# Which pairs of a feed-forward run as Strassen products, and in what order: one pair more, and a new order for the first

## The chip, the cores and the metric

The kernel runs on one core of a Trainium2 chip. The metric is the device time of one execution in microseconds, the median of several runs; smaller is better.

## The reference, cut to what matters

One layer over 640 tokens (512 of a prompt, 128 of eight running streams) of width 1024: a feed-forward, a mixer, a second feed-forward, each behind a modulated RMS norm, and a final norm. The change touches the two feed-forwards alone.

```python
D_MODEL, D_FF = 1024, 2816
def swiglu(h, w1, w2):
    g, u = jnp.split(h @ w1, 2, axis=-1)
    return (jax.nn.silu(g) * u) @ w2
...
        hn = modulate(rmsnorm(x, norm_g[l, 0]), sh1, sc1)
        x = x + 0.5 * g1[:, None, :] * swiglu(hn, ffn_w1[l, 0], ffn_w2[l, 0])
...
        hn = modulate(rmsnorm(x, norm_g[l, 2]), sh3, sc3)
        x = x + 0.5 * g3[:, None, :] * swiglu(hn, ffn_w1[l, 1], ffn_w2[l, 1])
```

## The kernel before, in words

Everything is held transposed: a tile is 128 features by 640 tokens, two halves of 320 columns. Every product of float32 numbers is made of three fast ones: a number is split into a high part (a rounded copy, made by ScalarE) and a low part (the rest, a subtraction on VectorE), and TensorE adds high times high, high times low and low times high.

**A feed-forward** is `ffn(fi)` for fi 0 and 1. Its 2816 hidden features are 22 **pairs** (`p`, 0 to 21): one 128-wide column block of g and the same of u. The pairs stand in six parts (`PARTS` 4, 4, 4, 4, 3, 3); after the pairs of a part come eight "down" products (`first_downs`, `down`) which multiply the part's hidden tiles by w2 and are added to x. A pair's weights come as one job of 1 MB into one of two buffers `raw0`, `raw1`; SyncE loads the next job when the low parts of the last block of the job before the previous one have been made (`load_job`, a wait on `blk_lo`). The weights are cut into **blocks** of 128x512. Block b has its high and low part in one of seven slots; ScalarE makes the high part (`blk`, L1569) when TensorE has done with block b - 7 and counts `blk_hi`; VectorE makes the low part (`blk`, L2142) and counts `blk_lo`; TensorE counts `blk_done`.

**Two kinds of pair.** The first `PLAIN` = 3 pairs are plain: four blocks, 8 k-tiles x 3 terms x 2 halves x 2 outputs = 96 matmuls of 320 columns (L1056, L1075). From pair 3 on a pair is in Strassen's form (Winograd's variant, `wino_pair`): the pair is a 2x2 product (g and u by first and second half of the tokens; the inner dimension split in two), and seven products of 12 matmuls each (`product`, L1087) take the place of eight. For this VectorE makes four sums of weight blocks per pair (`s_add`, L2105: s1w, a difference in the raw buffer, s2w, and another in the raw buffer, counted by `s_sum`), and, once per feed-forward, sums of activations: `t_sums(fi, kk)` for kk 0 to 3 (four operations of 128x320 each, L2278 to L2283) with their splits `t_high`, `t_low`, `t1_high`, `t1_low`, counted by `t_ready`. The products are added up in three PSUM banks: x (a half of pC, in turn for even and odd pairs), z (a half of acc0) and w (the other half of acc0). ScalarE copies partial states of the banks out (the **snapshots** s0, p7, s1, s2, L1750, counted by `snap`), and VectorE adds these to banks: c21, c22, c11 (L2350, L2353, L2357, counted by `c_sum`). Then come silu on ScalarE (L1762, L1764), the product with u on VectorE (L2362, `hidp_done`), and its split, `hid_high` (L1719) and `hid_low` (L2306).

**What sets the order.** Each engine works strictly through its own list, and these lists are written out by hand in the `plain_pair`, `wino_pair` and `ffn` of the four engines; semaphores join them. In `wino_pair` ScalarE and VectorE make the blocks of the next pair (b + 7 to b + 13) in between the snapshots and sums of this one. Two waits of TensorE matter here: the second product of a pair writes acc0 and waits until c11 of the pair before has been made (`c_sum` 3n; the z bank and w bank are read by c21 and c11), and the third product, on the x bank, waits for the snapshot s0 of the same pair (`snap` 4n + 1).

**Duos.** In some pairs (`DUO_ROWS`; in the first feed-forward after pairs 1, 2, 5, ...; in the second after 3 and 7) TensorE also computes two chunks of the conditioning vectors: `duo_rows` (L986) after the pair, `duo_row` on ScalarE (L1702, last in its list for the pair, counted by `d_row`), then two transposes `duo_cols` (L997) within the next pair, which wait for `d_row`, and `duo_sum` on VectorE.

Of the kernel before, what the change touches and what calls it, by code (L numbers as in the profile page):

```python
# [8 lines left out]
ALU = mybir.AluOpType  # L9
# [19 lines left out]
PLAIN = 3  # L29
KQ = KD // 2  # L30
# [54 lines left out]
def trunk_program(nc, x_prompt, x_sample, state_ssm, state_conv, c_prompt, c_sample, w_ada, b_ada, norm_g,  # L85
# [347 lines left out]
    SLOT0, RAW0 = (2, 4), (0, 1)  # L433
    BLOCK = {}
    for p, b in enumerate(BLK_PAIR):
        for j in range(4 if p < PLAIN else SLOTS):
            BLOCK[b + j] = ("plain" if p < PLAIN else "wino", p, j)
# [20 lines left out]
    def slot_of(fi, b, lo, cols):  # L458
        return slots[(b + SLOT0[fi]) % SLOTS][:, lo * WB:lo * WB + cols]
# [20 lines left out]
    S_AT = {1: 2, 2: 3, 4: 1, 6: 4}  # L480
# [367 lines left out]
    def _(pe):  # L848
# [231 lines left out]
        def product(fi, b, out, block, first):  # L1080
# [3 lines left out]
            for kk in range(KQ):  # L1084
                a_hi, a_lo = block(kk)
# [5 lines left out]
        def wino_pair(fi, p, cols):  # L1091
# [14 lines left out]
            if cols is not None and p == PLAIN:  # L1106
                duo_cols(cols)
# [5 lines left out]
            if p == PLAIN:  # L1113
                pe.wait_ge(t_ready, 6 * fi + KQ + 2)
# [420 lines left out]
    def _(act):  # L1535
# [18 lines left out]
        def blk(fi, b):  # L1554
# [4 lines left out]
            if kind == "wino" and j in S_AT:  # L1559
                act.wait_ge(s_sum, 4 * wino_before(fi, p) + S_AT[j])  # L1560
# [160 lines left out]
        def plain_pair(fi, p):  # L1721

            b = BLK_PAIR[p]
            if p == 1:
                t_high(fi, 1)
# [4 lines left out]
            if p == 1:  # L1730
                t_high(fi, 2)
            if p == 2:
                t_high(fi, 3)
            blk(fi, b + 7)
            blk(fi, b + 8)
            act.wait_ge(blk_done, fi * NB + b + 4)
            if p == PLAIN - 1:
                t1_high(fi)
            hid_high(fi, p)
            blk(fi, b + 9)  # L1740
            blk(fi, b + 10)

        def wino_pair(fi, p):
# [8 lines left out]
            blk(fi, b + 7)  # L1752
            snapshot("p7", z_bank, 2)
            blk(fi, b + 8)
            snapshot("s1", x, 3)
            blk(fi, b + 9)
            blk(fi, b + 10)
            snapshot("s2", x, 5)
# [287 lines left out]
    def _(dve):  # L2046
# [779 lines left out]
```

## Time and profile before

| | us |
|---|---|
| median of 3 runs (lowest to highest) | 1442.93 (1442.92 to 1444.68) |
| the profiled execution | 1445.51 |
| its span in the trace | 1443.9 |
| TensorE busy in matmuls | 1422.3 (99%) |
| VectorE busy | 1014.5 (70%) |
| ScalarE busy | 663.6 (46%) |
| GpSimd busy | 71.5 (5%) |

The span is from the first to the last instruction in the trace; the device time holds some 1.6 us more around it. The shares are means over the whole span. A timeline row gives start, length, engine, line, operation, tiles, count, and in brackets how long the engine was idle before it and what ended that. Operations on one engine overlap a little, so that what a step costs in a dense stretch is the distance from its start to the next start, not its own length. The first feed-forward's part 0 lies at 22 to 124 us, the second's at 986 to 1076 us.

### The profile page before, as it was taken

The page shows a single profiled execution, that of the slowest core. Times are in us where ns is not written, and L with a number is a line of the kernel's source. Part 1 is how long each engine was busy: PE and PEld are TensorE (multiplying, and loading weights), DVE is VectorE, ACT ScalarE, POOL GpSimd, SP SyncE. Part 2 cuts the span into 40 slices and gives each one's busy share as a digit, 9 for nine tenths or more (in the row PEclk, how much of TensorE's full clock was granted, in tenths as well). Part 3 has the DMA queues.
Part 4 walks back from the last instruction along what each step waited for, and adds up shares of the span by engine and source line. Part 5 has one row for each costly group of instructions (what it writes and reads, how often), then busy time and mean ns, then how long its engine had stood idle before and what let it go on. Part 6 is the DMA issues. An engine that isn't in the chain of part 4 may idle for free.

```text
span 1443.9 us, 25671 instructions
## 1 busy us (share of the span) xinstructions
PE 1422.3 (99%) x10202; PEld 1372.2 (95%) x10202; DVE 1014.5 (70%) x1742; ACT 663.6 (46%) x1186; POOL 71.5 (5%) x121
## 2 busy tenths in 40 slices
PE   7999999999999999999999999999999999999998
PEld 6899999999999999999789999998999999999997
DVE  5767677676776776667886567557767676767776
ACT  5543525253435444666825453226425253444354
POOL 3100000000000130000100000004000000000001
PEclk9999999999999999999999999999999999999999
DMA  9752434444344612231362222444324233231222
GB/s 319 213 187 61 159 105 146 117 147 147 110 139 132 184 30 74 74 93 54 98 187 77 67 73 63 133 143 122 110 56 143 67 88 88 71 105 52 81 74 74
DMA packets 219564, 161.02 MB, mean 112 GB/s; under 512 B 6858, under 2 KB 204678, under 8 KB 219458
## 3 DMA queue, kind: packets, MB, share of 16 engines
q1 hardware_dynamic: 217490, 153.89, 35.7%
q0 software_dynamic: 1696, 5.56, 1.3%
q8 instruction: 74, 1.21, 0.4%
q14 instruction: 32, 0.26, 0.1%
q10 hardware_dynamic: 272, 0.10, 0.0%
HBM read 151.50 MB, written 8.03 MB: 110 GB/s over the span
## 4 chain that ended last, share of the span: by engine, by line
PE 92%; DVE 3%; DMA 2%; ACT 1%; POOL 1%; issue 1%; SPq 0%; DVEq 0%; ACTq 0%; POOLq 0%
PE acc L864 25%; PE acc L1196 19%; PE pC L1087 18%; PE acc L1087 14%; PE acc L1075 4%; PE pB L986 2%; PE acc L1145 2%; PE pC L1336 1%; DMA ada_raw<-in_w_ada 1%; DMA raw<-in_ffn_w 1%; PE pB L945 1%; PE pB L1321 1%; PE pC L1471 1%; PE pC L1355 1%; PE acc L881 0%
## 5 line engine op out<-in xcount | busy, mean ns | idle before, releaser
L1569 ACT ACTIVATE slot<-raw 128x512 fp32r<-128x512 f32 (+1 forms) x310 | 189.7, 616 | 239.4 <-PE acc L1196 137.8
L2142 DVE TENSOR_TENSOR slot<-raw,slot 128x512 fp32r<-128x512 f32 (+1 forms) x310 | 208.6, 677 | 53.8 <-ACT slot L1569 51.3
L1196 PE MATMUL acc<-hid_hi,slot 128*128 128x320 f32 x1240 | 238.5, 310 | 0.0
L1087 PE MATMUL pC<-hn_hi,slot 128*128 128x320 f32 x912 | 216.3, 309 | 0.0
L1196 PEld LDWEIGHTS acc<-hid_hi,slot 128*128 128x128 f32 x1240 | 195.1, 188 | 2.9 <-issue 2.1
L864 PE MATMUL acc<-hn_hi,whi 128*128 128x320 f32 x672 | 161.5, 322 | 0.0
L1087 PEld LDWEIGHTS pC<-hn_hi,slot 128*128 128x128 f32 x912 | 156.2, 188 | 2.5 <-issue 2.5
L864 PE MATMUL acc<-hn_hi,wlo 128*128 128x320 f32 x672 | 153.5, 310 | 0.0
L864 PE MATMUL acc<-hn_lo,whi 128*128 128x320 f32 x672 | 153.5, 310 | 0.0
L1087 PE MATMUL acc<-tT,slot 128*128 128x320 f32 x912 | 146.3, 309 | 0.0
L1196 PE MATMUL acc<-hid_lo,slot 128*128 128x320 f32 x620 | 142.0, 308 | 0.0
L1087 PE MATMUL pC<-hn_lo,slot 128*128 128x320 f32 x456 | 140.8, 309 | 0.0
L1087 PEld LDWEIGHTS acc<-tT,slot 128*128 128x128 f32 x912 | 136.5, 188 | 0.0
L864 PEld LDWEIGHTS acc<-hn_hi,whi 128*128 128x128 f32 x672 | 112.4, 189 | 6.4 <-issue 5.9
L864 PEld LDWEIGHTS acc<-hn_lo,whi 128*128 128x128 f32 x672 | 112.9, 189 | 0.0
L864 PEld LDWEIGHTS acc<-hn_hi,wlo 128*128 128x128 f32 x672 | 112.8, 189 | 0.0
L1196 PEld LDWEIGHTS acc<-hid_lo,slot 128*128 128x128 f32 x620 | 103.8, 188 | 0.0
L2086 DVE TENSOR_TENSOR xadd<-acc,gate 128x128 f32<-128x128 f32 x95 | 27.6, 290 | 90.4 <-PE acc L1196 77.4
L2056 DVE TENSOR_TENSOR wlo<-wraw,whi 128x1024 fp32r<-128x1024 f32 x50 | 61.0, 1222 | 38.5 <-ACT whi L1549 37.9
L1087 PEld LDWEIGHTS pC<-hn_lo,slot 128*128 128x128 f32 x456 | 85.5, 188 | 0.0
L2080 DVE SCALAR_TENSOR_TENSOR xT<-acc,gate,xT 128x320 f32<-128x320 f32 (+1 forms) x190 | 82.6, 475 | 0.2 <-PE acc L881 0.2
L1087 PE MATMUL pC<-tT,slot 128*128 128x320 f32 x456 | 73.2, 309 | 0.0
(389 smaller groups left out, 2404.3 us busy)
## 6 DMA issues: line engine op xcount, KB each, us to landing
raw<-in_ffn_w SPq DMA_DIRECT2D x86, 512.0 KB, 5.1
sraw<-in_w_ada SPq DMA_DIRECT2D x26, 1024.0 KB, 7.2
wraw<-in_w_in SPq DMA_DIRECT2D x36, 512.0 KB, 3.6
raw<-in_ffn_w SPq DMA_DIRECT2D x16, 1024.0 KB, 5.0
ada_raw<-in_w_ada SPq DMA_DIRECT2D x8, 1024.0 KB, 11.0
wraw<-in_w_out SPq DMA_DIRECT2D x16, 512.0 KB, 4.2
raw<-in_ffn_w SPq DMA_DIRECT2D x8, 768.0 KB, 4.4
sraw<-in_w_ada_final SPq DMA_DIRECT2D x6, 1024.0 KB, 7.5
```

The source lines that it names most:

```text
L864: last = mm(acc[p][:, h * BANK:h * BANK + HALF], w[:, k, :], a[:, k * TOK + h * HALF:k * TOK + (h + 1) * HALF], start=(k == 0 and t == 0), ...
L945: last = nc.tensor.transpose(out[:, c * P:(c + 1) * P], src[:, c * P:(c + 1) * P], ident[:, :])
L986: last = mm(q_rows[lane_of(duo)][q * QUAD:(q + 1) * QUAD, :], c_f32[:, k, :], kxn(duo_raw(duo, j), KD, ADA_COLS)[:, k, :], start=(kk == 0) ...
L1075: last = mm(half(acc[d], h), w[:, kk * P:(kk + 1) * P], a[:, k * TOK + h * HALF:k * TOK + (h + 1) * HALF], start=(k == 0 and t == 0), stop ...
L1087: last = mm(out, w[:, kk * P:(kk + 1) * P], a, start=(first and kk == 0 and t == 0), stop=(kk == KQ - 1 and t == 2), skip_group_check=not ...
L1145: last = mm(a[h], w[t // 2][:, k, :], (hid_hi, hid_lo)[t % 2][:, k * TOK + h * HALF:k * TOK + (h + 1) * HALF], start=(k == 0 and t == 0), ...
L1196: last = mm(a[h], w[t // 2][:, k, :], (hid_hi, hid_lo)[t % 2][:, k * TOK + h * HALF:k * TOK + (h + 1) * HALF], start=(k == 0 and t == 0), ...
L1569: A(slot_as(fi, b, 0), source_of(fi, b), ACT.Copy).then_inc(blk_hi, 1)
L2056: V.tensor_tensor(out=weights(n, i, 1, w), in0=wraw[p][:, 0:w], in1=weights(n, i, 0, w).bitcast(F32), op=ALU.subtract).then_inc(wlo_done, 1)
L2080: return V.scalar_tensor_tensor(out=x[:, s:e], in0=a[s // HALF][:, p:p + e - s], scalar=gate[:, q, f * GRP:f * GRP + 1], in1=x[:, s:e], op ...
L2086: V.tensor_tensor(out=by_stream(xadd[:, SEQ:TOK]), in0=by_stream(a[1][:, SEQ - HALF:HALF]), in1=g, op=ALU.mult)
L2142: V.tensor_tensor(out=slot_as(fi, b, 1), in0=source_of(fi, b), in1=slot_as(fi, b, 0).bitcast(F32), op=ALU.subtract).then_inc(blk_lo, 1)
```

## The change

`PLAIN` goes from 3 to 2: pair 2 is a Strassen pair as well, in both feed-forwards. As the sums of activations must now be there one pair earlier, they are made during pairs 0 and 1, and pair 2, the first Strassen pair, has an order of its own: first the two products that need no activation sum (b11 and b21), then t2 (waiting tile by tile), t3, t1, t4 and b22; its blocks are numbered in that order (`FIRST_ROLES`), and its snapshots follow in the order in which the banks must be free (s0, s1, p7, s2). `hid_high` and `hid_low` of pair 1 and its product with u move behind the start of pair 2. The slots are numbered anew so that the last blocks fall where they fell.

```diff
-PLAIN = 3
+PLAIN = 2
...
-    SLOT0, RAW0 = (2, 4), (0, 1)
+    SLOT_OF, RAW0 = ((0, 1, 2, 3, 6, 4, 5), (4, 5, 6, 0, 1, 2, 3)), (0, 1)
+    FIRST_ROLES = (0, 5, 2, 1, 4, 3, 6)
...
@@ TensorE, wino_pair
             if p == PLAIN:
                 pe.wait_ge(silu_done, fi * N_PAIR + p)
-                pe.wait_ge(t_ready, 6 * fi + KQ)
-            elif PART_OF[p] != PART_OF[p - 1]:
+                product(fi, b + 1, w_bank, b21, True)
+                if cols is not None:
+                    duo_cols(cols)
+                pe.wait_ge(snap, 4 * n + 1)
+                product(fi, b + 2, x, t2, False, 6 * fi)
+                product(fi, b + 3, z_bank, t3, True)
+                pe.wait_ge(snap, 4 * n + 2)
+                pe.wait_ge(t_ready, 6 * fi + KQ + 2)
+                product(fi, b + 4, x, t1, False)
+                pe.wait_ge(snap, 4 * n + 3)
+                product(fi, b + 5, z_bank, t4, False)
+                pe.wait_ge(snap, 4 * n + 4)
+                product(fi, b + 6, x, b22, False)
+                return
+            if PART_OF[p] != PART_OF[p - 1]:
...
@@ ScalarE, wino_pair
             snapshot("s0", x, 1)
+            if p == PLAIN:
+                blk(fi, b + 3)
+                blk(fi, b + 4)
+                snapshot("s1", x, 3)
+                blk(fi, b + 5)
+                blk(fi, b + 6)
+                snapshot("p7", z_bank, 4)
+                hid_high(fi, p - 1)
+                blk(fi, b + 7)
+                snapshot("s2", x, 5)
+                blk(fi, b + 8)
+                blk(fi, b + 9)
+                blk(fi, b + 10)
...
@@ VectorE, wino_pair
+            if p == PLAIN:
+                blk(fi, b + 4)
+                gated_pair(fi, p - 1)
+                blk(fi, b + 5)
+                hid_low(fi, p - 1)
+                blk(fi, b + 6)
+                if cols is not None:
+                    duo_sum(cols)
+                blk(fi, b + 7)
+                dve.wait_ge(blk_done, fi * NB + b + 6)
...
             V.tensor_tensor(out=c21, in0=snaps["s1"], in1=z_bank, op=ALU.add).then_inc(c_sum, 1)
+            if p == PLAIN:
+                blk(fi, b + 8)
+                blk(fi, b + 9)
             blk(fi, b + 10)
```

In `product` the new argument makes t2 wait for `t_ready` before each k-tile. `plain_pair` on VectorE now holds, for pair 0, both t_sums 0 and 1; for pair 1, s1w, t_sums 2, s2w, t_sums 3, their splits, the raw difference, `t1_low` and one block. Pair 3 follows pair 2 as any Strassen pair follows another, with the waits on `c_sum` and `snap` above.

VectorE, from the last two blocks of the first Strassen pair of feed-forward 0 to its hidden product. `slot<-raw` with the line of `blk` is the low part of a block, `s1w`, `s2w` and `raw<-raw` are the weight sums, `tmp1<-rT,acc0`, `tmp1<-rT,sq` and `tmp0<-sq,acc0` are c21, c22 and c11. Before, in pair 3 (the pair ahead of the down products of part 0):

```order
L2142 TENSOR_TENSOR slot2<-raw0,slot2 128x512 [waits blk_hi]
L2350 TENSOR_TENSOR tmp1<-rT,acc0 128x320 [waits hid_ready,snap,blk_done]
L2142 TENSOR_TENSOR slot3<-raw0,slot3 128x512 [waits blk_hi]
L2353 TENSOR_TENSOR tmp1<-rT,sq 128x320 [waits snap]
L2142 TENSOR_TENSOR slot4<-raw1,slot4 128x512 [waits blk_hi]
L2357 TENSOR_TENSOR tmp0<-sq,acc0 128x320 [waits hidp_done,blk_done]
```

Of the change, in pair 2:

```order
L2342 TENSOR_TENSOR hid_lo<-tmp1,hid_hi 128x640 [waits hhi_ready]
L2176 TENSOR_TENSOR slot0<-raw0,slot0 128x512 [waits blk_hi]
L2127 TENSOR_TENSOR s1w<-raw1 128x512 [waits blk_lo,raw_in1]
L2127 TENSOR_TENSOR raw1<-raw1 128x512 [waits s_sum]
L2176 TENSOR_TENSOR slot1<-raw1,slot1 128x512 [waits blk_hi]
L2399 TENSOR_TENSOR tmp1<-rT,acc0 128x320 [waits hid_ready,blk_done]
L2127 TENSOR_TENSOR s2w<-s1w,raw1 128x512 [waits s_sum,blk_lo]
L2176 TENSOR_TENSOR slot3<-s2w,slot3 128x512 [waits blk_hi]
L2127 TENSOR_TENSOR raw1<-raw1,s2w 128x512 [waits blk_lo,s_sum]
L2405 TENSOR_TENSOR tmp1<-rT,sq 128x320 [waits snap]
L2176 TENSOR_TENSOR slot4<-s1w,slot4 128x512 [waits blk_hi]
L2410 TENSOR_TENSOR tmp0<-sq,acc0 128x320 [waits hidp_done]
```

Rows are left out between these (low parts of further blocks and a duo's sum). Ahead of c11 there now stand the low part of hidden tile 1, that of this pair's last block, all four sums of the next pair and five of its low parts.

ScalarE, from the snapshot p7 of the first Strassen pair of feed-forward 0 to the snapshot s0 of the next. `sq<-acc0` is p7, `rT<-pC` s2, `sq<-pC` s0, `tmp0<-tmp0` and `tmp0<-pC` the two halves of silu, `srow<-pB` the row of a duo. Before there is no Strassen pair behind pair 3 in part 0. Of the change, in pairs 2 and 3:

```order
L1758 ACTIVATE sq<-acc0 128x320 [waits blk_done]
L1731 ACTIVATE hid_hi<-tmp1 128x640 [waits hidp_done]
L1581 ACTIVATE slot1<-raw1 128x512 [waits blk_done,raw_in1]
L1758 ACTIVATE rT<-pC 128x320 [waits blk_done]
L1784 ACTIVATE tmp0<-tmp0 128x320 [waits c_sum]
L1786 ACTIVATE tmp0<-pC 128x320 [waits blk_done]
L1581 ACTIVATE slot0<-raw1 128x512 [waits blk_done,s_sum]
L1714 ACTIVATE srow<-pB 128x256 [waits d_tr,d_mm]
L1758 ACTIVATE sq<-pC 128x320 [waits blk_done]
```

Left out are five blocks ahead of the silu, and the pair's own `hid_hi` behind the block `slot0<-raw1`. The duo's row and the next snapshot s0 stand behind silu, which waits for c11, and behind that `hid_hi`, which waits for VectorE's hidden product.

## Rows read from the trace of the kernel before

**Rows 1.** The page: span, busy time by engine, the chain by engine.

```profile
span 1443.9 us, 25671 instructions
PE 1422.3 (99%) x10202; PEld 1372.2 (95%) x10202; DVE 1014.5 (70%) x1742; ACT 663.6 (46%) x1186; POOL 71.5 (5%) x121
PE 92%; DVE 3%; DMA 2%; ACT 1%; POOL 1%; issue 1%; SPq 0%; DVEq 0%; ACTq 0%; POOLq 0%
```

**Rows 2.** The chain in order of time: start, length, what.

```profile
49.95 14.31 PE acc L1075 x96
64.26 1.86 PE pB L986 x32
66.13 14.29 PE acc L1075 x96
...
131.36 1.76 PE pC L1087 x12
133.12 1.76 PE acc L1087 x12
```

**Rows 3.** Waits of TensorE: for whom, us, times, longest.

```profile
PE acc L1145 <- DVE hid_lo L2306: 0.7, 1, 0.7
```

**Rows 4.** Timeline of ScalarE at the end of pair 3, feed-forward 0.

```profile
95.18 1.15 ACT L1569 ACTIVATE slot<-raw 128x512 fp32r<-128x512 f32 x2 [2.99 <-DMA raw<-in_ffn_w]
```

**Rows 5.** Timeline of VectorE in pair 4 of feed-forward 0.

```profile
134.15 0.69 DVE L2142 TENSOR_TENSOR slot<-s1w,slot 128x512 fp32r<-128x512 f32 x1
134.92 0.49 DVE L2357 TENSOR_TENSOR tmp<-sq,acc 128x320 f32<-128x320 f32 x1
...
136.25 0.69 DVE L2105 TENSOR_TENSOR s1w<-raw 128x512 f32<-128x512 f32 x1
136.97 0.69 DVE L2105 TENSOR_TENSOR raw<-raw 128x512 f32<-128x512 f32 x1
137.58 0.82 DVE L2362 TENSOR_TENSOR tmp<-tmp 128x640 f32<-128x640 f32 x1
138.32 0.68 DVE L2142 TENSOR_TENSOR slot<-raw,slot 128x512 fp32r<-128x512 f32 x1
```

**Rows 6.** Timeline of TensorE: second product of pair 5, feed-forward 0.

```profile
138.23 1.92 PE L1087 MATMUL acc<-tT,slot 128*128 128x320 f32 x12
```

**Rows 7.** Timeline of ScalarE in pair 4 and at the start of pair 5.

```profile
135.51 0.45 ACT L1762 ACTIVATE tmp<-tmp 128x320 f32<-128x320 f32 x1
136.67 0.44 ACT L1764 ACTIVATE tmp<-pC 128x320 f32<-128x320 f32 x1 [0.70 <-PE pC L1087]
137.01 0.62 ACT L1569 ACTIVATE slot<-raw 128x512 fp32r<-128x512 f32 x1
138.43 0.74 ACT L1719 ACTIVATE hid_hi<-tmp 128x640 fp32r<-128x640 f32 x1 [0.80 <-DVE tmp L2362]
139.08 0.42 ACT L1750 ACTIVATE sq<-pC 128x320 f32<-128x320 f32 x1
```

**Rows 8.** Timeline of VectorE and ScalarE, pair 2 and 3: a duo's sum, a duo's row.

```profile
81.18 0.19 DVE L2244 TENSOR_TENSOR modc<-pB,b_col 128x36 f32<-128x36 f32 x1
81.40 0.20 DVE L2245 TENSOR_TENSOR modc<-pB,modc 128x36 f32<-128x36 f32 x1
83.44 0.36 ACT L1702 ACTIVATE srow<-pB 128x256 f32<-128x256 f32 x1
```

**Rows 9.** The end: TensorE's last matmuls, and busy time with TensorE's clock by stretch.

```profile
1435.74 1.04 PE L1171 MATMUL acc<-ident,sraw 128*128 128x128 f32 x8
1435.00:1440.00 5.00, 1.77 (x17) 1.53 (x15) 5.00 (x9) 1.25 (x2) 0.00 (x0) 1.00 0.80 295
1440.00:1444.00 4.00, 0.00 (x0) 0.00 (x0) 1.17 (x2) 0.00 (x0) 0.00 (x0) 0.60 0.77 287
```

More of the change, by code:

```diff
@@ L1078, in plain_pair, with product @@
                     last.then_inc(blk_done, 1)
-        def product(fi, b, out, block, first):
+        def product(fi, b, out, block, first, groups=None):
             pe.wait_ge(blk_lo, fi * NB + b + 1)
@@ L1084, in product @@
             for kk in range(KQ):
+                if groups is not None:
+                    pe.wait_ge(t_ready, groups + kk + 1)
                 a_hi, a_lo = block(kk)
@@ L1729, in plain_pair @@
                 t_high(fi, 0)
[L1730 to L1741, printed above, removed]
+                blk(fi, b + 7)
+                t_high(fi, 1)
+                hid_high(fi, p)
+                blk(fi, b + 8)
+                return
+            t_high(fi, 2)
+            blk(fi, b + 5)
+            t_high(fi, 3)
+            blk(fi, b + 6)
+            t1_high(fi)
         def wino_pair(fi, p):
@@ L1751, in wino_pair @@
             snapshot("s0", x, 1)
[L1752 to L1758, printed above, removed]
+            if p == PLAIN:
[11 more added lines that the diff above has]
+                blk(fi, b + 10)
+            else:
+                blk(fi, b + 7)
+                snapshot("p7", z_bank, 2)
+                blk(fi, b + 8)
+                snapshot("s1", x, 3)
+                blk(fi, b + 9)
+                blk(fi, b + 10)
+                snapshot("s2", x, 5)
             blk(fi, b + 11)
@@ L2131, in blk @@
                 first_sums(fi, b)
-                if j == 1:
-                    if n:
-                        dve.wait_ge(blk_lo, last_low[2])
-                    dve.wait_ge(s_sum, 4 * n + 2)
-                    s_add(s2w[:, :], s1w[:, :], w[:, 0:WB], ALU.subtract)
+                if j == 1 and p > PLAIN:
+                    third_sum(fi, b)
                 if j == 3:
@@ L2277, in t_sums @@
             a, b, n = hn_f(kk), hn_f(kk + KQ), 3 * (KQ * fi + kk)
+            if kk >= 2:
+                dve.wait_ge(t_ready, 6 * fi + kk - 1)
             V.tensor_tensor(out=t1_f(kk), in0=half_of(a, 1), in1=half_of(a, 0), op=ALU.subtract).then_inc(t_sum, 1)
@@ L2313, in plain_pair @@
                 t_sums(fi, 0)
-            if p == 1:
                 t_sums(fi, 1)
+                gated_pair(fi, p)
+                t_low(fi, 0)
+                blk(fi, b + 7)
                 t_low(fi, 1)
-                t_sums(fi, 2)
-            if p == 2:
-                t_sums(fi, 3)
-                t_low(fi, 3)
+                hid_low(fi, p)
+                blk(fi, b + 8)
+                return
+            first_sum(fi, b + 4)
+            t_sums(fi, 2)
+            third_sum(fi, b + 4)
@@ L2335, in plain_pair @@
[L2335 to L2348 removed]
+                if cols is not None:
+                    duo_sum(cols)
+                blk(fi, b + 9)
```

97 lines of the change are left out of this document (50 added, 47 removed).

## Prediction

> **What bounds the kernel now.** I read the page first: TensorE is busy 99% of the span and takes 92% of the chain that ended last [rows 1]. So time comes out only where TensorE has fewer matmuls to do, and goes in only where it is made to stand. Then the chain in order of time around the stage that changes: a plain pair is a row of 96 matmuls and 14.3 us, a product of a Strassen pair a row of 12 and 1.76 us, so 7 x 1.76 = 12.3 us a pair, or 0.147 us a matmul [rows 2]. Then the waits of TensorE: in the feed-forwards it hardly waits at all, the largest being 0.7 us in the first down products of part 0 [rows 3]. VectorE, at 70%, looks as if it had room, but that is a mean over the span; the question is whether it and ScalarE have room between pairs 0 and 3, where the change puts more work into less time, and what is queued ahead of the few results on which TensorE waits.
>
> **What is taken away.** 96 matmuls become 84, twice: 24 matmuls x 0.147 = 3.5 us, all on TensorE and so on the path. The 0.7 us wait goes too, for another reason. It began with ScalarE, idle for 2.99 us until the second job of down weights had landed [rows 4], with silu of pair 3 queued behind. That load follows a duo of 2 MB, which SyncE issues when the duo rows behind pair 2 are done, and itself waits for the last low part of pair 3's own blocks. The changed pair 2 ends about 1.8 us earlier, and those low parts are made in its course, while ScalarE will, as shown below, need the job later. I take 0.6 us for it. Together -4.1 us.
>
> **What is added, and hidden.** Three more blocks in each feed-forward (a high and a low part each) and four weight sums more: on ScalarE 3 x 0.52, on VectorE 7 x 0.61 = 4.3 us. This is beside TensorE's work as long as VectorE keeps its lead. In the opening of pair 2 it does: t2 is the third product, and counting VectorE's new list through pairs 0 and 1 with steps of 0.60 (128x512), 0.74 (128x640) and 0.40 us (128x320), the fourth activation sum is split about 3 us before TensorE asks for it. The seventh product's low part comes about 1 us before its turn (its place is in the count below). So I cost the opening at nothing; if it were late by a step, that is 0.6 us.
>
> **What becomes a new wait: c11.** The second product of pair 3 writes acc0 and must wait for c11 of pair 2. Before, no Strassen pair followed another in part 0, and pairs 4 and 5 show how it normally goes: c11 starts at 134.92 and ends at 135.41 [rows 5], the second product of pair 5 starts at 138.23 [rows 6]: 2.8 us to spare. In the new list of pair 2 that margin is used up. I count from the moment the fourth product of pair 2 ends (time 0), since p7's snapshot waits for it. ScalarE: p7, next start after 0.35; hid_high of pair 1, 0.74 long as in [rows 7], done at 1.1. VectorE then has, one behind the other (steps as between starts in [rows 5]: 0.61 for a 128x512 step, 0.72 where a sum waits for the sum ahead of it, 0.74 for 128x640, 0.40 for 128x320):
> - hid_low 1.1, low part of the last block 1.9, s1w 2.5, raw difference 3.2, low 3.8, c21 4.4,
> - s2w 4.8, low 5.4, low of s2w 6.2 (after its high part on ScalarE: s2w ends at 5.5, high part 0.63), raw difference 6.8, low 7.4,
> - c22 8.0, low 8.4, c11 9.0, ending at 9.5.
>
> The low part of the last block ends at 2.6, and its product starts at 3.5: the 1 us named above.
>
> **Feed-forward 1** has no duo there. TensorE wants acc0 after products 5, 6, 7 and the first of pair 3: 4 x 1.76 = 7.0. It stands 9.5 - 7.0 = 2.5 us. And it stands again: the third product waits for snapshot s0 of pair 3, which on ScalarE is behind silu, hid_high and a block. From c11's end at 9.5: silu 0.35 + 0.45 (10.3), VectorE's hidden product 0.82 (11.1), hid_high 0.74 (11.9), s0 0.42 (12.3) [rows 5, 7]. TensorE has finished the second product at 9.5 + 1.76 = 11.3: another 1.0 us. In all 3.5 us.
>
> **Feed-forward 0** has duo rows behind pair 2, 1.86 us more of work [rows 2], so acc0 is wanted at 8.9; and a duo's sum in VectorE's list, 0.25 us [rows 8], so c11 ends at 9.8. That alone would be 0.9 us. But before the second product TensorE has the duo's two transposes, which wait for the duo's row, last in ScalarE's list for pair 2: c11 9.8, silu 10.6, hidden product 11.4, hid_high 12.2, row 0.37 [rows 8] 12.5. TensorE stands 12.5 - 8.9 = 3.6 us; by then s0 follows at once, and no second wait comes.
>
> Behind pair 3 everything is as it was, and I find no later wait that would take the 7.1 us up: TensorE leads the chain to the end.
>
> **Sum.** -3.5 - 0.6 + 3.6 + 3.5 = +3.0 us, against the profiled span of 1443.9 (1445.51 with what lies around it). The median of the runs is 1442.93, 2.6 us under the profiled run, so the forecast is 1445.9 us. Two hundredths of a per cent this way or that decide on which side of 0.2% (2.9 us, about what a measurement of this kernel can tell from no change) it falls. Both stands come from chains of some 15 steps; an error of 0.03 us a step, for semaphores, makes 0.5 us in each.
>
> **Bounds of what the trace does not show.** No row shows a Strassen pair behind this new list. From below: VectorE's list is not waited for at all (the 2.8 us of margin as in pair 5), stands 0 and 0. From above: every step by its full length (0.69, 0.82, 0.49) and not by the distance of starts, some 0.08 us more for 15 steps, 1.2 us more in each, and hence 5.4 us in all. I take the counted values, as [rows 5] show distances of starts for these very operations, back to back.
>
> **A rule that speaks against the change more strongly.** TensorE's clock: at the end of the kernel the last matmul ends at 1436.8; the clock stands at 1.00 up to 1440 and at 0.60 in the mean from 1440 to 1444 [rows 9]. With its two levels (2.4 and 1.2 GHz, 1.0 and 0.5) the mean means that it fell near 1440.8, 4.0 us after the last matmul. The forecast stand of 3.6 us in feed-forward 0 is close to that. The Trainium skill, "TensorE: Matmul & The Clock Gate", section on the clock gate, says that the default is the throttled clock and that idleness brings it back; by that rule the matmuls behind the stand would run at half speed for a while, and by the trace, which has no stand of 3 us in midst of its work, nothing is seen yet.
>
> **Rivals.**
> - *The clock falls in the stand of feed-forward 0* (slower still). After 4.0 us it fell, after 3.6 us it may. Price: a matmul takes 0.147 us more, a product 1.8 us; for one to four products 1.8 to 7 us, so 1447.7 to 1453, mostly 1449. For it: the nearness of 3.6 to 4.0. Against: one sample, and it is on the longer side. It would show as a clock under 1.00 and products of 3.5 us behind the stand.
> - *VectorE and ScalarE keep up* (faster). If c11 of pair 2 is made within 6.0 us of the fourth product, nothing stands: acc0 is free by 7.0, and s0 and the duo's row, 2.8 us behind c11, come by 8.8, when they are wanted. Then 1442.9 - 4.1 = 1438.8 us. For it: 70% and 46% busy [rows 1], and 2.8 us of margin in pair 5. Against: the list has 13 steps ahead of c11 with sizes that the trace gives to 0.01 us; they would have to be a third shorter. Between 6.0 and 9.5 each us costs one or two.
> - *Only the duo's wait counts*: feed-forward 0 stands for 3.6 us, feed-forward 1 not, so 1442.4, no change. Against: the same list is in both, and acc0 is wanted earlier in the second. I hold it inside the first case's lower end.
>
> **How the numbers follow.** Forecast case 0.78 (1443.4 to 1448.4 for errors of the count in both directions and for the scatter of medians, which for the kernel before is 1.8 us between runs); keeping up 0.12; clock 0.10. The range of 8 in 10 leaves out the faster case and the far end of the clock: 1442.5 to 1449.0. Slower by over 0.2%, above 1445.8: a little over half of the first case, 0.41, and the clock's 0.10: 0.51. Within 0.2%: the rest of the first, 0.37. Faster: 0.12.
>
> **What would show it.** Right: TensorE idle once near 82 us for 3.5 us, released by ScalarE's row of a duo, and twice near 1033 and 1038 us, 2.5 us for c11 and 1.0 us for a snapshot; 24 matmuls fewer; the 0.7 us wait in the first down products gone; c11 of pair 2 some 9.5 us behind the fourth product. Wrong: no such waits, or one in the opening of pair 2 on `t_ready` or a block; or the clock below 1.00 behind 82 us.

## The result, and the profile after

| | before | after |
|---|---|---|
| median (lowest to highest), 6 runs each | 1444.49 (1442.92 to 1444.68) | 1452.18 (1447.58 to 1453.34) |
| the profiled execution | 1445.51 | 1447.58 |
| its span | 1443.9 | 1446.0 |

The ratio is 1.005, with a 95% interval of 1.004 to 1.006: slower, by 7.7 us. The forecast was +3.0 us. Two things stand out before any row is read. The median of before itself is now 1444.5, where three runs had given 1442.9; and the six runs of after scatter over 6 us. Their mean granted TensorE clocks go with their times: 0.998 for 1447.58, 0.997 for 1449.04, 0.993 or 0.994 for the four between 1452.15 and 1453.34. The execution that was profiled is the fastest of the six, so its trace can't show the whole loss.

The page of after, against [rows 1]:

```profile
span 1446.0 us, 25675 instructions
PE 1419.7 (98%) x10178; PEld 1369.6 (95%) x10178; DVE 1025.1 (71%) x1762; ACT 670.2 (46%) x1202; POOL 71.3 (5%) x121
PE 91%; DVE 3%; ACT 1%; DMA 1%; POOL 1%; issue 1%; SPq 0%; DVEq 0%; ACTq 0%; POOLq 0%
```

24 matmuls fewer, as meant, and TensorE's share of the chain down by one per cent. The waits of TensorE (for whom, us in total, times, longest):

```profile
PE pB L998 <- ACT srow L1714: 3.5, 1, 3.5
PE acc L1090 <- DVE tmp L2410: 2.5, 1, 2.5
```

Both are new, and the 0.7 us of [rows 3] is gone. The other waits are those of before, but for two outside the changed pairs: the one for a transfer of conditioning weights, near 40 us, went from 1.6 to 0.7 us, and one of 0.3 us near 748 us is new. In the timeline of TensorE the new waits stand in pair 3 of feed-forward 0 and of feed-forward 1:

```profile
85.99 0.44 PE L998 MATMUL pB<-ident,srow 128*128 128x128 f32 x2 [3.51 <-ACT srow L1714]
86.18 2.01 PE L1090 MATMUL acc<-tT,slot 128*128 128x320 f32 x12
88.03 1.92 PE L1090 MATMUL pC<-tT,slot 128*128 128x320 f32 x12
...
1035.59 2.84 PE L1090 MATMUL acc<-tT,slot 128*128 128x320 f32 x12 [2.51 <-DVE tmp L2410]
1038.37 2.70 PE L1090 MATMUL pC<-tT,slot 128*128 128x320 f32 x12
1040.91 1.92 PE L1090 MATMUL acc<-tT,slot 128*128 128x320 f32 x12
```

In feed-forward 0 the products behind the wait start 1.8 us apart, as always. In feed-forward 1 two products take 2.8 and 2.5 us from start to start. The table by stretch (the number before the last two is the granted clock) says why:

```profile
82.00:86.00 4.00, 0.49 (x5) 0.23 (x3) 3.54 (x7) 2.39 (x6) 0.00 (x0) 1.00 1.04 346
86.00:90.00 4.00, 4.00 (x28) 4.00 (x29) 2.00 (x4) 1.76 (x5) 0.00 (x0) 1.00 1.08 367
...
1034.00:1038.00 4.00, 2.41 (x12) 2.42 (x12) 3.56 (x7) 2.06 (x5) 0.00 (x0) 0.81 0.01 4
1038.00:1042.00 4.00, 4.00 (x22) 3.66 (x22) 2.21 (x3) 2.58 (x6) 0.00 (x0) 0.76 0.70 242
```

The clock fell to its lower level (1.2 GHz, 0.50) behind the shorter wait, in feed-forward 1, and stayed at 1.00 behind the longer one. A clock of 0.81 over 4 us means 1.5 us at half speed, 0.76 means 1.9 us: 3.4 us in all, in which 1.7 us of work is lost. I call this a fall. It begins at about 1036.5 us, 0.9 us after TensorE has gone back to work at 1035.59. The snapshot wait of 1.0 us that was forecast near 1038 us isn't to be seen, since the slowed second product covers it.

The chains of VectorE and ScalarE came out as counted. In feed-forward 1 the fourth product of pair 2 ends near 1025.9 us (the fifth starts at 1025.88); then, on the two engines:

```profile
1026.08 0.44 ACT L1758 ACTIVATE sq<-acc 128x320 f32<-128x320 f32 x1 [0.18 <-PE acc L1090]
...
1035.05 0.48 DVE L2410 TENSOR_TENSOR tmp<-sq,acc 128x320 f32<-128x320 f32 x1
```

c11 ends at 1035.5, 9.6 us behind the fourth product (counted: 9.5). In feed-forward 0, ScalarE:

```profile
83.24 0.47 ACT L1784 ACTIVATE tmp<-tmp 128x320 f32<-128x320 f32 x1 [1.80 <-DVE tmp L2410]
...
84.92 0.74 ACT L1731 ACTIVATE hid_hi<-tmp 128x640 fp32r<-128x640 f32 x1 [0.37 <-DVE tmp L2415]
85.57 0.37 ACT L1714 ACTIVATE srow<-pB 128x256 f32<-128x256 f32 x1
```

silu, hid_high and the duo's row, 3.5 us behind TensorE's demand at 82.5. So the waits, less what was taken away, explain the +3 us of the forecast; the rest varies between executions.

### The profile page after: what moved, and what is told of

Its sections match the earlier page's. It is cut to its first block, busy times and chain, and to the rows that moved or that the text cites. A ratio compares the mean times of both kernels' runs of the same rounds, so it can differ in the third digit from the quotient of the medians.

```text
span 1446.0 us, 25675 instructions
## 1 busy us (share of the span) xinstructions
PE 1419.7 (98%) x10178; PEld 1369.6 (95%) x10178; DVE 1025.1 (71%) x1762; ACT 670.2 (46%) x1202; POOL 71.3 (5%) x121
## 4 chain that ended last, share of the span: by engine, by line
PE 91%; DVE 3%; ACT 1%; DMA 1%; POOL 1%; issue 1%; SPq 0%; DVEq 0%; ACTq 0%; POOLq 0%
PE acc L865 24%; PE acc L1208 19%; PE pC L1090 19%; PE acc L1090 14%; PE acc L1157 2%; PE acc L1076 2%; PE pB L987 2%; PE pC L1348 1%; DMA ada_raw<-in_w_ada 1%; PE pB L946 1%; PE pB L1333 1%; PE pC L1483 1%; PE pC L1367 1%; PE acc L882 0%; POOL hnf L788 0%
## 5 line engine op out<-in xcount | busy, mean ns | idle before, releaser
L1090 PE MATMUL pC<-hn_hi,slot 128*128 128x320 f32 x960 | 227.8, 310 | 0.0
L1090 PEld LDWEIGHTS pC<-hn_hi,slot 128*128 128x128 f32 x960 | 164.5, 188 | 2.9 <-issue 2.9
L1090 PE MATMUL acc<-tT,slot 128*128 128x320 f32 x960 | 155.0, 310 | 2.5 <-DVE tmp L2410 2.5
L1090 PE MATMUL pC<-hn_lo,slot 128*128 128x320 f32 x480 | 148.3, 309 | 0.0
L1090 PEld LDWEIGHTS acc<-tT,slot 128*128 128x128 f32 x960 | 144.4, 189 | 2.8 <-DVE tmp L2410 2.8
L1090 PEld LDWEIGHTS pC<-hn_lo,slot 128*128 128x128 f32 x480 | 90.1, 188 | 0.0
L2102 DVE SCALAR_TENSOR_TENSOR xT<-acc,gate,xT 128x320 f32<-128x320 f32 (+1 forms) x190 | 82.5, 475 | 0.2 <-PE acc L882 0.2
L1090 PE MATMUL pC<-tT,slot 128*128 128x320 f32 x480 | 77.7, 311 | 0.0
```

The costliest lines, as they stand in the source:

```text
L1090: last = mm(out, w[:, kk * P:(kk + 1) * P], a, start=(first and kk == 0 and t == 0), stop=(kk == KQ - 1 and t == 2), skip_group_check=not ...
L2102: return V.scalar_tensor_tensor(out=x[:, s:e], in0=a[s // HALF][:, p:p + e - s], scalar=gate[:, q, f * GRP:f * GRP + 1], in1=x[:, s:e], op ...
```

## The experiments

Twelve kernels ran. Each had its own runs of before beside it on the same chip (medians 1444.06 to 1444.44). "The change" is the kernel after; waits are given in the order of the program. One execution of each kernel was profiled, so that what is said of the clock is known for that one execution.

### The change once more

> The change once more, unchanged, for a second profile and more times. Theory A (clock): the new stands of TensorE cost their own length (3.5 us in feed-forward 0, 2.5 and 1.0 in feed-forward 1) and, in most executions, the clock falls behind one or both of them, which costs some 2 to 5 us more. Then the median is 1452 +- 0.5, and a profile of 1452 us shows a granted clock under 1.00 behind 90 us as well as behind 1034 us, with the same waits. Rival B (something other than the clock varies, such as a transfer or a wait elsewhere): a profile of 1452 us shows the clock at 1.00 but for short stretches, and 5 us of waits that the first profile did not have. A profile near 1447.6 us would tell neither.

Median 1450.07 us (1448.96 to 1453.51, 5 runs), ratio 1.0044 (1.003 to 1.0057). The median is 1.4 us under the 1451.5 to 1452.5 that I expected. The profiled execution, at 1452.04, is one of the longer ones and can be read for the loss. TensorE in feed-forward 0:

```profile
86.33 0.69 PE L998 MATMUL pB<-ident,srow 128*128 128x128 f32 x2 [3.51 <-ACT srow L1714]
86.67 3.55 PE L1090 MATMUL acc<-tT,slot 128*128 128x320 f32 x12
90.02 2.73 PE L1090 MATMUL pC<-tT,slot 128*128 128x320 f32 x12
```

and by stretch:

```profile
82.00:86.00 4.00, 0.81 (x6) 0.55 (x4) 3.57 (x7) 2.05 (x5) 0.00 (x0) 0.87 0.99 323
86.00:90.00 4.00, 3.67 (x14) 3.67 (x15) 1.52 (x2) 1.12 (x4) 0.00 (x0) 0.50 1.08 363
90.00:94.00 4.00, 4.00 (x23) 4.00 (x23) 1.22 (x4) 1.91 (x4) 0.00 (x0) 0.77 0.29 103
...
1038.00:1042.00 4.00, 1.80 (x8) 1.80 (x9) 3.74 (x8) 1.82 (x5) 0.00 (x0) 0.84 0.01 4
1042.00:1046.00 4.00, 4.00 (x23) 4.00 (x22) 2.65 (x4) 2.80 (x7) 0.00 (x0) 0.73 0.55 179
```

The waits are the same to 0.01 us, 3.51 and 2.51. The clock is what differs: here it falls in the long stand too, at about 85.0, while TensorE stands, and comes back at 91.8. From the first product of pair 3 to the first down product it is 18.8 us (80.79 to 99.62), in the first profile 16.4 us (80.45 to 96.82): this fall costs 2.5 us. Most of the rest of the 4.4 us between the two spans is a fall of 3.4 us near 622 us, 1.7 us, at a place that the change doesn't touch (last section). Theory A held in kind, though not in its median, and rival B, other waits, is out.

### Filling the stands

```diff
+            if p == PLAIN + 1:
+                pe.wait_ge(hidp_done, fi * N_PAIR + PLAIN)
+                keep_clock((6, 4)[fi])
             if cols is not None and p > PLAIN:
                 duo_cols(cols)
...
             product(fi, b + 1, z_bank, t3, True)
+            if p == PLAIN + 1 and fi:
+                keep_clock(1)
             pe.wait_ge(snap, 4 * n + 1)
```

> The change, with TensorE kept busy in its stands of pair 3: six extra matmuls (128x256, result thrown away) ahead of the duo's transposes in feed-forward 0, four ahead of the wait for c11 and one ahead of the wait for snapshot s0 in feed-forward 1. They start when the hidden product of pair 2's predecessor is done, which is before the stand begins, and take the place of idle time, so the data arrive when they did. Theory A (clock): 1452.2 less the clock's share: the sum of the matmuls saved and the stands, 1444.5 + 3.0 = 1447.5 us (1446.5 to 1448.5), mean clock 0.998, waits of about 0.5, 0 to 0.5 and 0 to 0.5 us. Rival B (the clock is not what costs the rest): the idle time is filled but the data come as late, so 1452 us as for the change.

`keep_clock(n)` stands in the kernel before as well; it issues n matmuls whose result nobody reads. Median 1448.13 us (1446.58 to 1448.83, 8 runs), ratio 1.0024 (1.0014 to 1.0035), within the expected band. TensorE in feed-forward 0, profiled execution:

```profile
82.29 2.75 PE L1032 MATMUL acc<-upto,ident 128*128 128x256 f32 x12
85.97 0.44 PE L998 MATMUL pB<-ident,srow 128*128 128x128 f32 x2 [0.92 <-ACT srow L1719]
```

The profile counts each of the six matmuls twice. The transposes start at 85.97, as in after (85.99): the data came no earlier, TensorE merely worked in the meantime. The waits left were 0.9, 0.8 and 0.3 us, a little more than expected. The clock was 1.00 in all of 82 to 94 and 1034 to 1042 us. So work that does nothing made the kernel faster, 1448.1 against 1450.1 in the same series; the two intervals of the ratio touch, but the longest of the eight executions (1448.83) is shorter than the shortest of the change's five (1448.96).

To see which stand matters, each was filled alone: `keep_clock((6, 0)[fi])` without the single one, and `keep_clock((0, 4)[fi])`.

> The change with extra matmuls in the stand of feed-forward 0 alone (six of 128x256); the stands of feed-forward 1 stay. Theory A (the clock accounts for what is over 3.0 us): the clock stays at 1.00 between 84 and 92 us and falls behind the 2.5 us stand near 1036 us for a few us; median 1449.5 (1448.5 to 1450.5), between the 1448.1 with all stands filled and the 1450 to 1452 of the change. Rival B (only the stand of feed-forward 0 matters for the clock): 1448.1, the same as with all filled.

> The change with extra matmuls in the stands of feed-forward 1 alone (four and one); the stand of feed-forward 0 stays. Theory A: the clock falls behind the 3.5 us stand near 86 us and is 1.00 around 1036 us; median 1450.5 (1449.5 to 1451.5), as the longer stand brings the larger loss. Rival B (the fall in feed-forward 1 is what costs): 1448.1, the same as with all filled.

Feed-forward 0 filled: 1447.90 us (1446.71 to 1449.1, 8 runs), ratio 1.0026 (1.0015 to 1.0037). Feed-forward 1 filled: 1448.93 us (1448.58 to 1453.21, 5 runs), ratio 1.0039 (1.0025 to 1.0053). The first is as good as both filled, which is rival B's number and not the 1449.5 of theory A: the medians show no price of the fall in feed-forward 1, although the clock does fall there (0.64 and 0.50 at 1036 to 1040 us in that profile). The reason is the one seen above: the fall slows the second product, and TensorE would have waited for snapshot s0 behind it anyway. Without a fall (the profile of the kernel with the moved transposes, below, has none there) it is 4.65 us from the end of that stand to the fourth product, with one 5.32 us: 0.7 us, not 1.7. The second kernel shows two kinds of execution, three near 1448.7 and two at 1452.5 and 1453.2; the profiled one, of the second kind, had the clock at 0.50 from 86.5 to 93.3. The 1450.5 that I expected lies between the two kinds, and no execution had it.

### Taking the stands apart

c11 of pair 2 moved ahead on VectorE:

```diff
                 gated_pair(fi, p - 1)
                 blk(fi, b + 5)
+                dve.wait_ge(blk_done, fi * NB + b + 2)
+                dve.wait_ge(snap, 4 * n + 1)
+                dve.wait_ge(hidp_done, fi * N_PAIR + p)
+                V.tensor_tensor(out=c11, in0=snaps["s0"], in1=w_bank, op=ALU.add).then_inc(c_sum, 1)
                 hid_low(fi, p - 1)
```

At its old place, behind `blk(fi, b + 11)`, c11 is left out for pair 2.

> The change, with VectorE's c11 of pair 2 alone moved ahead, from behind the last blocks to right behind the last gated pair of pair 1. Counted in the rows' steps, the stand of feed-forward 0 goes from 3.5 to 2.9 us (it waits for the duo's row, which still stands behind silu, hidden product and hid_high), that of feed-forward 1 from 2.5 + 1.0 to about 1.5 + 1.3. Theory A (clock falls after stands near 2.5 us and more): time 1.4 us less by the waits, and the clock still falls in part of the executions; 1447 to 1451. If only stands over 3 us bring it down: 1446.1 us. Rival B (c11 isn't what was late; the late thing is c21, c22 or the blocks): waits unchanged, 1452.

```profile
PE pB L998 <- ACT srow L1714: 2.8, 1, 2.8
PE acc L1090 <- DVE tmp L2409: 1.5, 1, 1.5
PE pC L1090 <- ACT sq L1758: 1.0, 1, 1.0
```

Median 1446.87 us (1445.7 to 1449.19, 11 runs), ratio 1.0018 (1.0009 to 1.0027). The waits are 2.8, 1.5 and 1.0 us, where 2.9, 1.5 and 1.3 were counted; the late thing was c11. In the profile the clock fell with the end of the 2.8 us (0.62 over 86 to 90 us) and not behind the 1.5 us. But the profiled execution, 1449.19, is the longest of the eleven; the other ten are at 1445.7 to 1447.5, and the median is just under the 1447 to 1451 of theory A, nearer to the 1446.1 of a clock that doesn't fall. So a stand of 2.8 us can bring the fall, and in most executions it seems not to.

Duo 1's transposes moved behind the second product of pair 3:

```diff
-            if cols is not None and p > PLAIN:
+            if cols is not None and p > PLAIN + 1:
                 duo_cols(cols)
...
             product(fi, b + 1, z_bank, t3, True)
+            if cols is not None and p == PLAIN + 1:
+                duo_cols(cols)
             pe.wait_ge(snap, 4 * n + 1)
```

> The change with one thing moved on TensorE: in pair 3 of feed-forward 0 the two transposes of duo 1 stand behind the second product instead of ahead of it. Theory A (the 3.5 us are the duo's row, last in ScalarE's list, and the clock then falls in most executions): by the count, TensorE stands 0.9 us for c11 ahead of the second product and 0.9 us for the duo's row behind it, 1.8 us in place of 3.5, in two pieces that bring no fall of the clock near 86 us; feed-forward 1 stays as it is. So 1.7 us less by the waits and 2.7 us less in the executions that had the fall: median 1446.4 (1445.4 to 1447.4). Rival B (the wait goes with the list of VectorE whatever TensorE does first): the wait of 3.5 us stays in one piece at the second product, and the time at 1450 to 1452.

```profile
84.74 2.03 PE L1090 MATMUL acc<-tT,slot 128*128 128x320 f32 x12 [0.79 <-DVE tmp L2412]
87.47 0.44 PE L998 MATMUL pB<-ident,srow 128*128 128x128 f32 x2 [0.70 <-ACT srow L1716]
```

The 3.5 us became 0.8 and 0.7, as theory A has it, and the clock stayed at 1.00 from 82 to 94 us. The median, 1447.96 us (1445.13 to 1449.67, 12 runs; ratio 1.0023, 1.0014 to 1.0031), is 0.6 us above the expected band: the twelve fall into five of 1445.1 to 1446.4 and seven of 1447.8 to 1449.7. The profiled one (1448.15) had two falls elsewhere, at 42 and at 620 us, and none behind the 2.5 us stand of feed-forward 1, which was as long as ever; what the other six had isn't known.

Both moves together:

> The change with both small moves: duo 1's transposes behind the second product of pair 3, and VectorE's c11 of pair 2 right behind the last gated pair of pair 1. Counted: one wait of 1.1 us in feed-forward 0 (the duo's row), 1.5 and 1.3 us in feed-forward 1, no fall of the clock. 3.5 + 0.6 out, 1.2 + 2.8 in: the time of before, 1444.3 (1443.3 to 1445.3). Rival (waits near 1.5 us bring the clock down as well): falls at 0.50 near 1036 us and 1446 or more.

Median 1444.95 us (1443.75 to 1447.52, 11 runs), ratio 1.0007 (0.9998 to 1.0015), the waits 1.0 us in feed-forward 0 (1.1 counted) and 1.5 and 1.0 us in feed-forward 1 (1.5 and 1.3), the clock 1.00 at both places. Two moved steps bring the change from +0.5% to no difference from before.

### Stands of known length in the kernel before

Was it the stand alone that brought the clock down, or the work around it? In the kernel before, eight stands were put where nothing else changes, and their length set by GpSimd, which is idle there ([rows 1]: 5% busy). `STANDS` is 5, 7, 9, ... 19, and the range 2, 7, 10 (shown) or 15:

```diff
+        for i, p in enumerate(STANDS):
+            pool.wait_ge(blk_done, BLK_PAIR[p] + 5)
+            for j in range(10):
+                st.done(nc.gpsimd.memset(idle[:, :], 0.0))
+            nc.gpsimd.memset(idle[:, :], 0.0).then_inc(stand, 1)
...
             product(fi, b + 4, x, t1, False)
+            if fi == 0 and p in STANDS:
+                pe.wait_ge(stand, STANDS.index(p) + 1)
             product(fi, b + 5, w_bank, b21, True)
```

> The kernel before, with eight short stands of TensorE put into feed-forward 0 (pairs 5, 7, ... 19, ahead of the sixth product): GpSimd, idle there, waits for the fifth product, clears a small scratch tile three times and lets TensorE go on. Estimated length 0.9 to 1.2 us each, read from the profile. Theory A (the clock falls after stands of some 2.5 us or more only): time = before + 8 x length, about 1444.5 + 8 = 1453, no stretch with the clock under 1.00. Rival B (any stand can bring the clock down): stretches at 0.50 behind some of the eight, and more than 8 x length.

> The same, with the scratch tile cleared eight times, so that each stand is about 2.6 us (as the stand of feed-forward 1 in the changed kernel). Theory A: the clock falls behind a part of the eight stands, each time for about 2 to 4 us of work, which costs 1 to 3 us more; time = before + 8 x 2.6 = 1465 plus 8 to 16 us. Rival B (the clock's fall in the changed kernel has another cause than the stand, such as the work around it): 1465 and the clock at 1.00 behind all eight.

> The same, with the scratch tile cleared eleven times, so that each stand is about 3.6 us (as that of feed-forward 0 in the changed kernel). Theory A: the clock falls behind all or nearly all of the eight, for longer than behind stands of 2.6 us; time = before + 8 x 3.6 = 1473 plus 20 to 30 us. Rival B: 1473 and the clock at 1.00.

> The kernel before with eight stands of TensorE again, made longer: the scratch tile is cleared 16 times. The stands of the three kernels like it were 0.7, 1.7 and 2.35 us by the profile, 0.13 us for each clear beyond 0.7 or so, so I expect 3.5 us here, the length of the stand of feed-forward 0. Theory A: the clock falls in nearly all of the eight, early enough that a good part of the stand is already at half speed, and comes back after one or two spells of 3.4 us as seen after the 2.35 us stands; work at half speed for 2.5 to 6 us behind each. Time = 1444.4 + 8 x 3.5 = 1472.4 plus 8 x (1.3 to 3) = 1483 to 1496. Rival B (a stand of 3.5 us is like one of 2.35 us): plus 8 to 11 us, 1481 to 1483.

The waits of TensorE in the four profiles:

```profile
PE acc L1095 <- POOL idle L810: 5.5, 8, 0.7
```

```profile
PE acc L1095 <- POOL idle L810: 13.9, 8, 1.7
```

```profile
PE acc L1095 <- POOL idle L810: 18.8, 8, 2.4
```

```profile
PE acc L1095 <- POOL idle L810: 27.1, 8, 3.4
```

| stand | time (4 runs) | over before (1444.38; last 1444.14) | waits | left over | falls behind the eight stands, profiled execution |
|---|---|---|---|---|---|
| 0.7 us | 1450.66 | 6.3 | 5.5 | 0.8 | 0 |
| 1.7 us | 1460.45 | 16.1 | 13.9 | 2.2 | 0 |
| 2.35 us | 1474.07 | 29.7 | 18.8 | 10.9 | 5 |
| 3.4 us | 1487.92 | 43.8 | 27.1 | 16.7 | 7 |

The falls were matched to the stands by time: the five begin between 0.3 us ahead of TensorE's restart and 0.1 us behind it, the seven between 1.3 us ahead and 1.2 us behind. In the last three kernels the profiled execution is the fastest of the four. In the 1.7 us kernel (1458.92, mean clock 0.999, the others 0.997 or 0.998) falls in the others aren't excluded; the 0.7 us kernel has one fall, at 625 us, not behind a stand. The stands were shorter than I had estimated (0.7, 1.7 and 2.35 us for 0.9 to 1.2, 2.6 and 3.6); the fourth kernel's expectation uses the measured lengths. Between 1.7 and 2.35 us the left-over time goes from 0.3 to 1.4 us a stand. In the 2.35 us kernel a stand with a fall (first two rows) and one without (last two):

```profile
146.00:148.00 2.00, 1.31 (x5) 1.31 (x6) 0.06 (x1) 0.00 (x0) 0.47 (x4) 0.69 0.00 0
148.00:150.00 2.00, 2.00 (x9) 2.00 (x8) 0.00 (x0) 0.00 (x0) 0.00 (x0) 0.50 0.00 0
...
236.00:238.00 2.00, 1.13 (x8) 1.14 (x9) 0.23 (x1) 0.00 (x0) 0.60 (x4) 1.00 0.00 0
238.00:240.00 2.00, 2.00 (x16) 2.00 (x15) 0.83 (x2) 0.99 (x2) 0.00 (x0) 1.00 0.00 0
```

9 matmuls in 2 us against 16. DMA share is 0.00 in all of them, so no transfer has a part in it. The five falls hold the clock at 0.50 for 3.4 us each (17 us, 8.5 us of work); in the 3.4 us kernel five hold it for 3.4 and two for 6.8 us. That a stand alone brings the clock down, a longer one more often and for longer, is what theory A says, and the fourth kernel came out in its range (1483 to 1496, nearly all of the eight). The times expected of the second and third (1473 to 1481, 1493 to 1503) were missed, since their stands were too short: 1.7 us showed no fall, and what was expected of 2.6 us, a fall behind a part of the eight, came at 2.35 us.

### The same work in another order

If the loss is order alone, it can be had back without taking an operation out. VectorE's new list for pair 2, from the last gated pair on, in words (waits left out, the sums by name):

```text
gated_pair(fi, p - 1)
blk(fi, b + 5)
c11
hid_low(fi, p - 1)
blk(fi, b + 6)
duo_sum(cols), where there is one
blk(fi, b + 7)
c21, c22
blk(fi, b + 8)
hidden product (silu * u)
blk(fi, b + 9)
hid_low(fi, p)
blk(fi, b + 10) to blk(fi, b + 13)
```

ScalarE's list changes in pairs 2 and 3: silu of c11 right behind snapshot s2, then a block, silu's second half, a block, the duo's row and hid_high of pair 2; and pair 3's blocks b + 4 to b + 10 behind its first snapshot, between the others.

> The change with the same operations in another order on VectorE and ScalarE in pairs 2 and 3: c11 early, c21 and c22 behind the sixth product, then silu, hidden product, the duo's row and hid_high, with pair 3's blocks behind them and its snapshots in between. No operation is added or taken out. Counted in the rows' steps, feed-forward 0 has no stand in pair 3, feed-forward 1 two of 0.2 us. Theory (the loss is order: stands, and the clock that falls behind them): the 24 matmuls come out as 3.5 us, less 0.4, and the 0.7 us wait: 1444.5 - 3.0 = 1441.5 us (1440.5 to 1442.5), clock 0.998, no wait of TensorE over 0.5 us in pair 3. Rival (VectorE and ScalarE have too much work there, whatever the order): the stands move to other products or to pair 4, and the time stays above 1446.

TensorE in pair 3 of feed-forward 0, and the table by stretch there and in feed-forward 1:

```profile
82.44 0.38 PE L998 MATMUL pB<-ident,srow 128*128 128x128 f32 x2
82.58 2.01 PE L1090 MATMUL acc<-tT,slot 128*128 128x320 f32 x12
```

```profile
82.00:86.00 4.00, 4.00 (x30) 3.99 (x29) 2.90 (x5) 2.71 (x6) 0.00 (x0) 1.00 1.03 343
86.00:90.00 4.00, 4.00 (x30) 4.00 (x29) 3.50 (x9) 2.72 (x7) 0.00 (x0) 1.00 1.01 302
...
1034.00:1038.00 4.00, 4.00 (x29) 4.00 (x29) 3.92 (x8) 3.77 (x9) 0.00 (x0) 1.00 0.18 10
```

Median 1440.64 us (1440.29 to 1442.32, 11 runs), ratio 0.9976 (0.9967 to 0.9985): faster than before by 3.8 us and than the change, in the same series, by 9.4. No wait of TensorE in pair 3 is left, with VectorE busy for 3.92 of 4 us at the second place: it has the work to do that the rival said, and gets it done in time. From the start of pair 2 to the first down product of feed-forward 0 it is 27.2 us (65.98 to 93.2); before it was 29.0 (66.06 to 95.1), in the first profile of after 31.0 (65.86 to 96.8). That is 1.8 us less than before, the 12 x 0.147 us of the matmuls. In feed-forward 1, from the end of pair 0 to the first down product, it is 42.4 us (1002.05 to 1044.44) against 44.0 before (1003.82 to 1047.84), 1.6 us less.

Not all of the 3.8 us is order and matmuls. Of before's 24 times in this series seven lie at 1442.9 to 1443.2 and fifteen at 1444.35 to 1445.17; of this kernel's eleven, seven at 1440.3 to 1440.9 and four at 1441.7 to 1442.3. Low group against low group and high against high, the gain is about 2.5 us; the two profiles, each with one fall between 615 and 622 us, differ by 3.4 us in span (1443.9 and 1440.5). The rest goes with how often the high kind came up, of which the last section has more. VectorE's list and ScalarE's were changed together, so what each of them gave isn't known.

## Why the prediction was wrong

The forecast was 1445.9 us, with 1442.5 to 1449.0 for 8 in 10; it came out at 1452.18. By the steps:

- **Matmuls, -3.5 us.** Right. 24 fewer, and with the stands gone the two feed-forwards are 1.8 and 1.6 us shorter where they were changed.
- **The wait in the first downs, -0.6 us.** Right: it is gone. That its cause was the late job of weights rests on [rows 4] and was not tested by itself.
- **The opening of pair 2 at nothing.** Right. The first profile shows no wait of TensorE in it, and the profile of the reordered kernel none either.
- **Feed-forward 0, 3.6 us for the duo's row.** Right in size (3.51), in place (82 us) and in cause: moving the transposes behind one product split it into 0.8 and 0.7.
- **Feed-forward 1, 2.5 us for c11 and 1.0 us for s0.** Right. 2.51 us in both profiles; the 1.0 us hides under the slowed second product where the clock falls. Where it doesn't fall, in the kernel with the moved transposes, the wait is there: 0.8 us.
- **What failed: the clock.** The sum has no term for it, and the rival that has one was wrong in two steps. Its chance, 0.10, rested on one sample: the clock fell 4.0 us after the last matmul of the kernel [rows 9], and I read 3.6 us as on the safe side of it. In the second profile it fell about 2.2 us into the stand; with stands of 2.35 us in the kernel before, behind five of eight. One sample was too few: read in the same way in the other thirteen profiles, the clock falls 2.3 to 5.0 us after the last matmul. The shortest is that of the kernel with all stands filled (last matmul ends at 1437.85, clock at 1.00 up to 1440 us and 0.52 behind, so a fall at about 1440.15):

```profile
1436.81 1.04 PE L1188 MATMUL acc<-ident,sraw 128*128 128x128 f32 x8
1436.00:1440.00 4.00, 1.85 (x17) 1.61 (x15) 4.00 (x7) 1.30 (x2) 0.00 (x0) 1.00 0.71 266
1440.00:1444.00 4.00, 0.00 (x0) 0.00 (x0) 2.24 (x4) 0.00 (x0) 0.00 (x0) 0.52 1.03 383
```

The rival was also put in feed-forward 0 alone, while the stand of 2.5 us in feed-forward 1 had a fall in three of four profiles. Its price was right: "1.8 to 7 us" against 2.5 us measured for the fall in feed-forward 0 and 0.7 us net in feed-forward 1. Of the eleven executions of the change, six were at 1452.0 or more, with mean clocks of 0.993 or 0.994, five at 1450.1 or less, with 0.997 or 0.998; that the fall in the long stand divides them fits the one profile of each kind.
- **The base.** 1442.93 was the median of three runs that were of two kinds: with more runs 1444.1 to 1444.5. This put the forecast 1.6 us too low, while the profiled execution, 1445.51, from whose trace the terms were read, held a fall of its own.

Together, span against span, where each fall is known: the first profile is 1446.0 - 1443.9 = 2.1 us over before, and 3.0, plus 0.7 for the fall in feed-forward 1, less 1.7 for the fall near 619 us that before had and this execution hadn't, make 2.0. The second is 6.5 us over before, and 3.0 + 0.7 + 2.5 make 6.2. So the traces leave 0.1 and 0.3 us. That 1444.5 + 3.0 is just the first profile's 1447.58 is luck: that execution has a fall which isn't in the 3.0 and lacks one that before's profiled execution has.

Between medians the account is less complete: 1444.5 + 3.0 + 2.5 + 0.7 = 1450.7, and the remaining 1.5 us up to 1452.2 stays open. The profiled execution of before was itself 1.0 us over the median of its six others, and falls come at places that the change doesn't touch (near 42 us in three of the fourteen profiles, near 620 us, or where added stands shift it to, in seven; 1.7 us each); how often they come in a series is chance as far as these runs tell. The second series of the same kernel, with its median of 1450.1, doesn't ask for the 1.5 us.

## What to carry to other kernels

Where TensorE takes the whole of the time, price a new stand by its length and then ask whether the clock survives it: in the profiles of this kernel no fall was seen behind 0.7 us and 1.7 us, and falls behind five of eight stands of 2.35 us and seven of eight of 3.4 us, at 1.7 us or more of lost work each. Part of that can be hidden, in the stand itself or under a wait that comes anyway (2.5 and 0.7 us net here). A stand of 3.5 us can be worth splitting for the clock's sake; that this pays with the sum of the stands unchanged wasn't tried (the split here also shortened them, to 1.5 us). And a reordering that takes no operation out can be worth more (9.4 us here) than the arithmetic saved (3.5 us). When the runs of one kernel scatter, compare their mean granted clocks first, and profile until both kinds of execution have been seen; the trace of a short one explains only its own time.

## What was not expected of the hardware

**The fall is a matter of chance, for one and the same stand.** The 3.51 us stand kept the clock at 1.00 in one profile and lost it in another. Eight stands of 2.35 us gave five falls, eight of 3.4 us seven. Nor is the longest first: in one execution the 2.5 us stand had a fall and the 3.5 us stand not. The 2.5 us stand in turn had one in three profiles and none in a fourth, that of the moved transposes.

**It can come after the stand is over.** In the kernel with 3.4 us stands TensorE restarts at 238.59 and the clock is still 1.00; the table:

```profile
238.00:240.00 2.00, 1.42 (x9) 1.42 (x10) 0.00 (x0) 0.00 (x0) 0.42 (x3) 0.94 0.00 0
240.00:242.00 2.00, 2.00 (x9) 2.00 (x8) 0.54 (x2) 0.72 (x2) 0.00 (x0) 0.50 0.00 0
```

0.94 over two microseconds means that it fell at about 239.8, over 1 us into the work. The falls of these profiles last 3.4 us, those behind the longest stands at times 6.8 us. The Trainium skill, "TensorE: Matmul & The Clock Gate", section on the terms, puts the penalty at the throttled time times one less the ratio of the clocks, here a half. The kernel with 2.35 us stands agrees, with 18.8 us of waits and 20.5 / 2 = 10.2 us of lost work (3.4 us for each of the five falls and one more at 646 us) in a span 27.2 us longer than that of before, which itself has 1.7 us of them.

**A fall without any wait.** The kernel before has one, in the profiled execution, near 619 us:

```profile
612.00:616.00 4.00, 4.00 (x37) 3.81 (x35) 1.27 (x2) 2.77 (x3) 1.07 (x2) 1.00 0.10 23
616.00:620.00 4.00, 4.00 (x24) 3.78 (x24) 2.20 (x4) 1.76 (x5) 0.00 (x0) 0.77 0.42 106
620.00:624.00 4.00, 4.00 (x26) 4.00 (x25) 2.34 (x3) 3.97 (x11) 0.00 (x0) 0.80 0.67 174
```

TensorE doesn't wait there; from 609 to 618 us TensorE does small matmuls (of 8 to 128 columns, some 70 of them, and four of 512), and the clock falls at 618.2 us, for 3.4 us. Seven of the fourteen profiles have this fall, shifted by what the kernel did before it, and seven haven't, among them after, the kernel with all stands filled and that with 1.7 us stands. It costs 1.7 us, and the first six times of before do lie in two groups, 1442.9 and 1444.3 to 1444.7; that the fall is what divides them fits, but only one execution of before was profiled. That the small matmuls bring it is argued from the place alone; no run changed them. This stretch of the mixer is the next place to look for time in this kernel.
